# Latent attention's sums of squares: the rotated channels' squares are added before the matmul with ones

## The chip, the cores and the metric

The kernel runs on one core of one Trainium2 chip. Everything is float32; large weights are split into a high and a low part, and three matmuls (high by high, low by high, high by low) stand for one float32 product. The metric is the device time of one launch in microseconds (us). The kernel before took 1195.99 us as the median of three runs (1193.62 to 1198.3).

## The reference, cut to what matters

Two transformer layers over 256 tokens of 1024 channels. The part that is changed lies in the first layer's latent attention. Each of eight heads has queries and keys of 192 channels, 128 plain ones ("nope") and 64 that are rotated ("rope"), and each 192-vector is normalised before the rotation:

```
q_b = (rms_norm(cq, mla_cq_norm) @ w_uq).reshape(B, S, MLA_HEADS, MLA_QK_DIM)
k_b = concatenate([k_nope, broadcast_to(kr[:, :, None, :], (B, S, MLA_HEADS, MLA_ROPE_DIM))], axis=-1)
q_b = rms_norm(q_b, mla_q_norm)      # y = x * rsqrt(mean(x*x over 192) + 1e-6) * gain
k_b = rms_norm(k_b, mla_k_norm)
```

So each head and token needs one sum of 192 squares for the query and one for the key. The 64 rotated key channels are the same for all heads.

## The kernel before, in words

The program is written out by hand, engine by engine, in order. `latent_pe`, `latent_act`, `latent_dve` and `latent_pool` are the programs of TensorE, ScalarE, VectorE and GpSimd for the stage; what ties them together are semaphores (`wait_ge`, `then_inc`) and rings of buffers, where taking a buffer waits for the reader that had it last. Two rings of PSUM banks serve TensorE: `G` (three banks) for the projections, `M` (four banks) for the small products. Two SBUF rings of two buffers hold squares: `sq_ring` for the plain channels, `zt_ring` for the rotated query channels.

The stage has channels on partitions and tokens along the free dimension. A head pair `p` (0 to 3) has its plain channels in a tile of 128 partitions by 2 x 256 (two heads side by side), and its rotated channels in `mqr[:, p, :]`, 128 x 256: the even head's 64 channels on partitions 0 to 63, the odd head's on 64 to 127. The key's rotated squares `sqkr` are 128 x 256 with the same 64 channels in both halves.

TensorE goes through two loops of four turns:

- First loop, turn `half`: twelve matmuls of the key projection (`("ukv", 0)`, `mm_fm`, line 392), in turn 1 also the small product of `value_pe` (line 885), then the permutation for the rotation of query pair `half` (line 1109), then the sums of squares of query pair `half` (`mla_stat_pe`, lines 1131 and 1132).
- Second loop: twelve matmuls of the value projection (`("ukv", 1)`, `mm_tm`, line 410), then the sums of squares of key pair `half`. After the loop `ada_sums_pe(pe, 10)` (line 581), and then the next stage begins with 32 instructions of narrow scores (line 1489) and the gate projections (line 392).

ScalarE, for the query: squares the rotated channels (line 1178) and the plain ones (`mla_sq_act`, line 1140) of pair `half`, then turns the sums of pair `half - 1` into reciprocal roots (`mla_rstd_act`, Ln on line 1149, Exp on line 1151), then copies the key projection out of PSUM (line 1183). Between the loops it splits the next weights, of which the high part is written on line 344 (`next_hi(act, ("ukv", 1))`, which is the split of `("win", 7)`). In the second loop: square of key pair `half`, roots of the pair before, copy of the values (line 1191).

VectorE rotates the queries (lines 1237 to 1242), multiplies by the roots (lines 1248 to 1264), copies `value_pe`'s result (line 892), writes the low part of the split weights (line 351), and sums a modulation block (`ada_dve(dve, 10)`, lines 562 and 565). GpSimd has nothing to do in this stage before: its tables are made earlier, and its next instruction, a memset, waits for the stage's last `m_rope`.

A sum over partitions is a matmul with a matrix of ones. Before, each pair's sums take four float32 products of 256 columns, which accumulate in PSUM: for each of the two heads one of `ones` with the plain squares and one of `ones_lo` or `ones_hi` (ones on one half of the partitions) with the rotated squares.

Of the kernel before, what the change touches and what calls it, by code (L numbers as in the profile page):

```python
# [7 lines left out]
ALU = mybir.AluOpType  # L8
# [23 lines left out]
PT_, NPAR = _param_table()  # L32
CT_ = {}
NCON = 0
for _n, _k in [("ident", 128), ("ones_lo", 128), ("ones_hi", 128), ("perm64", 128), ("perm32", 128),
               ("cos", 256), ("sin", 256), ("cosr", 256), ("sinr", 256), ("mask2", 256), ("tri", 256),
               ("cadd", 30), ("cmul", 30), ("fold", 32)]:
    CT_[_n] = (NCON, _k)
    NCON += _k
# [108 lines left out]
def build(nc, ins, out):  # L148
# [130 lines left out]
    cmp_mm, cmp_set = sig("cmp_mm"), sig("cmp_set")  # L279
    ev_act, ev_dve = sig("ev_act"), sig("ev_dve")  # L280
    half_done = sig("half_done")
    m_sq, m_stat, m_nope, m_rope = sig("m_sq"), sig("m_stat"), sig("m_nope"), sig("m_rope")
    gt_exp, gt_set, gt_turn = sig("gt_exp"), sig("gt_set"), sig("gt_turn")
    cmp_sc, cmp_max, cmp_p, cmp_w = sig("cmp_sc"), sig("cmp_max"), sig("cmp_p"), sig("cmp_w")
# [775 lines left out]
    def latent_pe(pe):  # L1060
# [34 lines left out]
        for half in range(4):  # L1095
            b, old = G.take(ev_act("ukv", 0, half))
            if old:
                pe.wait_ge(*old)
            where["ukv", 0, half] = b
            mm_fm(pe, ("ukv", 0), ckvn, normed("vw") if half == 0 else held, b, half * 256,  # L1100
                  done=unit.hit("ukv", 0) if half == 3 else half_done.hit("ukv", 0, half))
            if half == 1:
                value_pe(pe)
            pm, old = M.take(rope_b("mq", half))
            if old:
                pe.wait_ge(*old)
            where["pm", "mq", half] = pm
            pe.wait_ge(*ev_act("uq", 2, half // 2))
            pe.matmul(pm[:, 0:256], cc("perm32"), mqr[:, half, :], start=True, stop=True).then_inc(
                perm_done.hit("mq", half), 1)  # L1110
            mla_stat_pe(pe, "mq", half, where["sqr", half][:, 0:256], ("ones_lo", "ones_hi"))
        for half in range(4):
            b, old = G.take(ev_act("ukv", 1, half))
            if old:
                pe.wait_ge(*old)
            where["ukv", 1, half] = b
            mm_tm(pe, ("ukv", 1), ckvn, held, b, half * 256, 256,
                  unit.hit("ukv", 1) if half == 3 else half_done.hit("ukv", 1, half))
            mla_stat_pe(pe, "mk", half, sqkr, ("ones_lo", "ones_lo"))
        ada_sums_pe(pe, 10)  # L1120

    def mla_stat_pe(pe, n, p, rsq, ones2):

        sm, old = M.take(rs_ln(n, p))
        if old:
            pe.wait_ge(*old)
        where["sm", n, p] = sm
        pe.wait_ge(*m_sq(n, p))
        sq = where["msq", n, p]
        for j in range(2):  # L1130
            pe.matmul(sm[:, j * 256:j * 256 + 256], ones[:], sq[:, j * 256:j * 256 + 256], start=True, stop=False)  # L1131
            ins_ = pe.matmul(sm[:, j * 256:j * 256 + 256], cc(ones2[j]), rsq, start=False, stop=True)
        ins_.then_inc(m_stat.hit(n, p), 1)

    def mla_sq_act(act, n, p, nope):
        buf, old = sq_ring.take(m_stat(n, p))
# [16 lines left out]
    def latent_act(act):  # L1153
# [16 lines left out]
        next_hi(act, ("ukv", 0))  # L1170
        hidden_act(act, 1)
        for half in range(4):
            buf, old = zt_ring.take(m_stat("mq", half))
            if old:
                act.wait_ge(*old)
            where["sqr", half] = buf
# [90 lines left out]
    def latent_pool(pool):  # L1267
        table_pool(pool, "mq", "mq_rope", "mq_rsw", "cosr", "sinr")
        table_pool(pool, "mk", "mk_rope", "mk_rsw", "cosr", "sinr")


    class Job:
# [1312 lines left out]
def _consts():  # L2585
    f = np.float32
# [5 lines left out]

    p = np.arange(128)
    put("ident", np.eye(128))
    put("ones_lo", (p < 64).astype(f)[:, None] * np.ones((1, 128), f))
    put("ones_hi", (p >= 64).astype(f)[:, None] * np.ones((1, 128), f))
    for n, h in (("perm64", 64), ("perm32", 32)):
        m = np.zeros((128, 128), f)
        m[p ^ h, p] = 1.0
# [158 lines left out]
```

## Time and profile before

| | us |
|---|---|
| median of three runs | 1195.99 |
| the profiled execution | 1199.0 |
| its span on the core | 1197.7 |
| TensorE busy | 1139.8 (95%) |
| VectorE busy | 748.5 (62%) |
| ScalarE busy | 590.9 (49%) |
| GpSimd busy | 25.9 (2%) |

The engine names in the rows are PE (TensorE matmul), PEld (its weight load), DVE (VectorE), ACT (ScalarE) and POOL (GpSimd). A matmul's duration in a timeline holds its way through the array, so that neighbours overlap; what one costs in a dense stretch is read from start to start, or from the chain of waits. A float32 product appears as two instructions. PEclk is the granted TensorE clock, 1.00 for 2.4 GHz and 0.50 for 1.2 GHz.

### The profile page before, as it was taken

How to read it: one execution, taken by the hardware profiler on the slowest of the kernel's cores; microseconds unless marked ns; L12 is line 12 of the kernel's file. 1: busy time of each engine (PE TensorE's matmuls, PEld its weight loads, DVE VectorE, ACT ScalarE, POOL GpSimd, SP SyncE). 2: the span in 40 equal slices, each digit the busy share in tenths (PEclk: the TensorE clock that was granted, in tenths of full speed). 3: DMA queues.
4: the chain of work that ended last, by engine and by line, in shares of the span. 5: the costliest groups of instructions: out<-in, count | busy, mean ns of one | idle time of the engine just before them, and what ended most of it. 6: DMA issues, size and time to landing. Idle time of an engine off the chain costs nothing.

```text
span 1197.7 us, 19285 instructions
## 1 busy us (share of the span) xinstructions
PE 1139.8 (95%) x7802; PEld 1033.5 (86%) x7802; DVE 748.5 (62%) x1411; ACT 590.9 (49%) x1043; POOL 25.9 (2%) x32
## 2 busy tenths in 40 slices
PE   7999699899899999999999899999999999999998
PEld 6987579788779999888988699998878978999986
DVE  2546546788658788765656666666455556666644
ACT  3455346444456666435325464444455357444533
POOL 0240000000000000001000000000000000000000
PEclk8999889899999999999989899999999989999999
DMA  7954563255144555564532275554545313655450
GB/s 310 384 187 179 219 247 141 92 199 212 62 141 159 179 187 193 183 248 173 195 108 102 70 267 195 191 177 159 193 146 178 116 62 130 214 181 189 141 193 36
DMA packets 30796, 207.81 MB, mean 174 GB/s; under 512 B 3539, under 2 KB 4051, under 8 KB 7156
## 3 DMA queue, kind: packets, MB, share of 16 engines
q1 hardware_dynamic: 30708, 206.58, 48.4%
q8 instruction: 62, 1.02, 0.3%
q14 instruction: 26, 0.21, 0.0%
HBM read 205.52 MB, written 1.05 MB: 172 GB/s over the span
## 4 chain that ended last, share of the span: by engine, by line
PE 84%; DVE 8%; ACT 4%; issue 2%; DMA 1%; SPq 0%; ACTq 0%; DVEq 0%
PE ps L392 47%; PE ps L1630 18%; PE ps L622 3%; PE ps L410 2%; DVE wlo L351 2%; DVE tm L565 1%; ACT whi L344 1%; PE ps L2231 1%; PE ps L2263 1%; DMA raw<-ada 1%; PE ps L1329 1%; PE ps L1755 1%; PE ps L581 1%; PE ps L1131 1%; PE ps L1407 1%
## 5 line engine op out<-in xcount | busy, mean ns | idle before, releaser
L351 DVE TENSOR_TENSOR wlo<-raw,whi 128x1024 fp32r<-128x1024 f32 (+2 forms) x328 | 370.3, 1171 | 253.3 <-ACT whi L344 253.1
L392 PE MATMUL ps<-H_h,whi 128*128 128x256 f32 x1552 | 447.9, 289 | 5.5 <-DVE wlo L351 5.5
L392 PE MATMUL ps<-H_l,whi 128*128 128x256 f32 x1552 | 442.5, 285 | 0.0
L392 PE MATMUL ps<-H_h,wlo 128*128 128x256 f32 x1552 | 442.3, 285 | 0.0
L344 ACT ACTIVATE whi<-raw 128x1024 fp32r<-128x1024 f32 (+2 forms) x328 | 315.5, 1010 | 184.8 <-PE ps L1630 111.9
L392 PEld LDWEIGHTS ps<-H_h,whi 128*128 128x128 f32 x1552 | 301.4, 194 | 10.4 <-issue 10.2
L392 PEld LDWEIGHTS ps<-H_l,whi 128*128 128x128 f32 x1552 | 301.4, 194 | 0.4 <-issue 0.2
L392 PEld LDWEIGHTS ps<-H_h,wlo 128*128 128x128 f32 x1552 | 301.2, 194 | 0.0
L1630 PE MATMUL ps<-whi,gl_h 128*128 128x512 f32 x264 | 105.6, 400 | 0.5 <-DVE wlo L351 0.5
L1630 PE MATMUL ps<-whi,gl_l 128*128 128x512 f32 x264 | 104.7, 396 | 0.0
L1630 PE MATMUL ps<-wlo,gl_h 128*128 128x512 f32 x264 | 104.6, 396 | 0.0
L1853 ACT ACTIVATE uw<-uw 128x256 f32<-128x256 f32 x66 | 27.4, 415 | 86.4 <-DVE uw L1944 86.4
L1630 PEld LDWEIGHTS ps<-whi,gl_h 128*128 128x128 f32 x264 | 49.7, 188 | 13.4 <-DVE wlo L351 1.4
L1630 PEld LDWEIGHTS ps<-wlo,gl_h 128*128 128x128 f32 x264 | 49.7, 188 | 12.1
L1630 PEld LDWEIGHTS ps<-whi,gl_l 128*128 128x128 f32 x264 | 49.7, 188 | 11.6
L1892 DVE SCALAR_TENSOR_TENSOR uw<-ps,par_sb,uw 128x255 f32<-128x255 f32 (+1 forms) x88 | 36.4, 475 | 25.2 <-ACT uw L1841 25.2
L1841 ACT ACTIVATE uw<-ps,par_sb 128x256 f32<-128x256 f32 x44 | 22.5, 562 | 46.5 <-PE ps L392 46.5
L565 DVE SCALAR_TENSOR_TENSOR tm<-raw,cs,tm 128x256 f32<-128x256 f32 x96 | 40.5, 477 | 0.0
L622 PE MATMUL ps<-H_h,whi 128*128 128x256 f32 x96 | 28.7, 299 | 4.9 <-DVE wlo L351 4.4
L1944 DVE TENSOR_TENSOR uw<-ps,rn 128x512 f32<-128x512 f32 x44 | 30.1, 684 | 2.2 <-PE ps L392 2.0
L1863 ACT ACTIVATE gl_h<-tm 128x256 fp32r<-128x256 f32 x66 | 27.5, 417 | 2.7 <-DVE tm L1859 2.7
L622 PE MATMUL ps<-H_l,whi 128*128 128x256 f32 x96 | 28.2, 294 | 0.0
(445 smaller groups left out, 1527.3 us busy)
## 6 DMA issues: line engine op xcount, KB each, us to landing
raw<-f SPq DMA_DIRECT2D x44, 1024.0 KB, 4.9
raw<-win SPq DMA_DIRECT2D x27, 1024.0 KB, 6.7
raw<-ada SPq DMA_DIRECT2D x24, 1024.0 KB, 5.8
raw<-up SPq DMA_DIRECT2D x22, 1024.0 KB, 4.8
raw<-g SPq DMA_DIRECT2D x20, 1024.0 KB, 4.9
raw<-pw SPq DMA_DIRECT2D x12, 1024.0 KB, 4.9
raw<-down SPq DMA_DIRECT2D x10, 1024.0 KB, 4.9
raw<-wa SPq DMA_DIRECT2D x4, 1024.0 KB, 9.6
```

What stands on the lines that cost most here:

```text
L344: act.activation(whi[j % NS][:, a:b], raw_of(key)[:, a:b], ACT.Copy).then_inc(w_hi.hit(key, half), 1)
L351: dve.tensor_tensor(wlo[j % NS][:, a:b], raw_of(key)[:, a:b], whi[j % NS][:, a:b].bitcast(F32), ALU.subtract).then_inc(w_lo.hit(key, half), 1)
L392: ins_ = pe.matmul(bank[:, m * 256:(m + 1) * 256], wt[a][:, kt * w + col + m * 128:kt * w + col + m * 128 + 128], act[b][:, k0 + kt, :], s ...
L410: ins_ = pe.matmul(bank[:, t * width:(t + 1) * width], act[b][:, kt, t * 128:(t + 1) * 128], wt[a][:, kt * w + col:kt * w + col + width], ...
L565: dve.scalar_tensor_tensor(out=o, in0=w, scalar=cs[:, kt:kt + 1], in1=o, op0=ALU.mult, op1=ALU.add).then_inc(ada_sum.hit(u, kt), 1)
L622: ins_ = pe.matmul(where["win", name][:, m * 256:(m + 1) * 256], wt[a][:, c:c + 128], H[b][:, k, :], start=k == 0 and m == 0 and i == 0, s ...
L1630: ins_ = pe.matmul(b[t][:], act[h][:, k0 + kt, t * 128:(t + 1) * 128], wt[a][:, kt * 512:(kt + 1) * 512], start=k0 + kt == 0 and i == 0 an ...
L1841: act.activation(w[:, m, :], z[:, m, :], ACT.Identity, bias=pc("b_conv", 2 * c + m), scale=pc("w_conv", (2 * c + m) * 3 + 2)).then_inc(u_i ...
L1853: act.activation(w[:, g, :], w[:, g, :], ACT.Silu).then_inc(u_silu.hit(n, c), 1)
L1863: act.activation(gl[0][:, c, :], where["tm", n, c][:, 0:256], ACT.Copy).then_inc(g_hi.hit(n, c), 1)
L1892: dve.scalar_tensor_tensor(out=w[:, m, s:], in0=z[:, m, 0:256 - s], scalar=pc("w_conv", (2 * c + m) * 3 + 2 - s), in1=w[:, m, s:], op0=ALU ...
L1944: dve.tensor_tensor(uw[c % 3][:], v2(where[n, c][:]), bc2(rn[:]), ALU.mult).then_inc(u_rn.hit(n, c), 1)
```

## The change

A new program part on GpSimd, `mla_add_pool`, adds the rotated squares onto the plain ones in place, for the even head on partitions 0 to 63 and for the odd head on 64 to 127: two additions of 64 x 256 for each pair, eight pairs. TensorE then needs one float32 product of 512 columns with `ones` for a pair in place of four of 256, and it asks for `m_add` (GpSimd's) in place of `m_sq` (ScalarE's). Each pair's product stands one turn later than before, key pair 3's behind `ada_sums_pe(pe, 10)`. The rotated query squares' buffers are free again when GpSimd has read them. Two constant matrices fall away, 256 columns of the constant table.

```diff
-for _n, _k in [("ident", 128), ("ones_lo", 128), ("ones_hi", 128), ("perm64", 128), ("perm32", 128),
+for _n, _k in [("ident", 128), ("perm64", 128), ("perm32", 128),
...
@@ latent_pe, first loop
-            mla_stat_pe(pe, "mq", half, where["sqr", half][:, 0:256], ("ones_lo", "ones_hi"))
+            if half:
+                mla_stat_pe(pe, "mq", half - 1)
@@ second loop
-            mla_stat_pe(pe, "mk", half, sqkr, ("ones_lo", "ones_lo"))
+            mla_stat_pe(pe, *(("mk", half - 1) if half else ("mq", 3)))
         ada_sums_pe(pe, 10)
+        mla_stat_pe(pe, "mk", 3)
...
-    def mla_stat_pe(pe, n, p, rsq, ones2):
+    def mla_stat_pe(pe, n, p):
...
-        pe.wait_ge(*m_sq(n, p))
-        sq = where["msq", n, p]
-        for j in range(2):
-            pe.matmul(sm[:, j * 256:j * 256 + 256], ones[:], sq[:, j * 256:j * 256 + 256], start=True, stop=False)
-            ins_ = pe.matmul(sm[:, j * 256:j * 256 + 256], cc(ones2[j]), rsq, start=False, stop=True)
-        ins_.then_inc(m_stat.hit(n, p), 1)
+        pe.wait_ge(*m_add(n, p))
+        pe.matmul(sm[:], ones[:], where["msq", n, p][:], start=True, stop=True).then_inc(m_stat.hit(n, p), 1)
+
+    def mla_add_pool(pool, n, p):
+
+        sq, r = where["msq", n, p], sqkr if n == "mk" else where["sqr", p][:, 0:256]
+        pool.wait_ge(*m_sq(n, p))
+        for a, b in ((0, 0), (64, 256)):
+            ins_ = pool.tensor_tensor(sq[a:a + 64, b:b + 256], sq[a:a + 64, b:b + 256], r[a:a + 64, :], ALU.add)
+        ins_.then_inc(m_add.hit(n, p), 1)
@@ latent_act
-            buf, old = zt_ring.take(m_stat("mq", half))
+            buf, old = zt_ring.take(m_add("mq", half))
@@ latent_pool
+        for n in ("mq", "mk"):
+            for p in range(4):
+                mla_add_pool(pool, n, p)
```

How TensorE's queue stands at the end of the first loop's turn 1. Before, with `sq1` the plain and `zt1` the rotated squares of query pair 1, `ps` a PSUM bank and `con_sb` the table with the half ones:

```order
L885 MATMUL ps1<-cw21_112,hid2_125 15x128 x3
L1109 MATMUL ps5<-mqr_93,con_sb_50 128x256 [waits ev_act,rs_ln]
L1131 MATMUL ps6<-sq1_68,ones_54 128x256 [waits m_sq,cmp_hid]
L1132 MATMUL ps6<-zt1_76,con_sb_50 128x256
L1131 MATMUL ps6<-sq1_68,ones_54 128x256
L1132 MATMUL ps6<-zt1_76,con_sb_50 128x256
L392 MATMUL ps2<-ckvn_h_121,whi1_62 128x256 [waits w_lo,ev_act]
```

The same place now:

```order
L886 MATMUL ps1<-cw21_112,hid2_125 15x128 x3
L1110 MATMUL ps4<-mqr_93,con_sb_50 128x256 [waits ev_act,gt_set]
L1132 MATMUL ps5<-sq0_67,ones_54 128x512 [waits m_add,rs_ln]
L393 MATMUL ps2<-ckvn_h_121,whi1_62 128x256 [waits w_lo,ev_act]
L393 MATMUL ps2<-ckvn_l_122,whi1_62 128x256
```

Four products of pair 1 have become one, twice as wide, and it is pair 0's (`sq0`). At the end of the stage, before:

```order
L1131 MATMUL ps6<-sq1_68,ones_54 128x256 [waits m_sq,rs_ln]
L1132 MATMUL ps6<-arow0_82,con_sb_50 128x256
L1131 MATMUL ps6<-sq1_68,ones_54 128x256
L1132 MATMUL ps6<-arow0_82,con_sb_50 128x256
L581 MATMUL ps2<-tm0_71,ones_54 128x256 [waits ada_sum,ev_act]
L581 MATMUL ps2<-tm1_72,ones_54 128x256
L1489 MATMUL ps3<-kcn_98,q_87 128x15 [waits rope_set,cmp_set,rs_ln]
```

and now:

```order
L1132 MATMUL ps5<-sq0_67,ones_54 128x512 [waits m_add,rs_ln]
L582 MATMUL ps2<-tm0_71,ones_54 128x256 [waits ada_sum,ev_act]
L582 MATMUL ps2<-tm1_72,ones_54 128x256
L1132 MATMUL ps6<-sq1_68,ones_54 128x512 [waits m_add,rs_ln]
L1499 MATMUL ps3<-kcn_98,q_87 128x15 [waits rope_set,cmp_set,rs_ln]
```

Key pair 3's product has moved behind the modulation sums (line 581 before, 582 now) and stands directly in front of the next stage. ScalarE's and VectorE's queues keep their order. GpSimd's has, between the tables and the memset, sixteen additions, of which the first four rows are:

```order
L1139 TENSOR_TENSOR sq0_67<-sq0_67,zt0_75 64x256 [waits m_sq]
L1139 TENSOR_TENSOR sq0_67<-sq0_67,zt0_75 64x256
L1139 TENSOR_TENSOR sq1_68<-sq1_68,zt1_76 64x256 [waits m_sq]
L1139 TENSOR_TENSOR sq1_68<-sq1_68,zt1_76 64x256
```

Each pair's first addition waits for ScalarE's square of the plain channels; nothing stood there before.

## Rows read from the trace of the kernel before

**Rows 1.** The page's parts on busy time and on granted clock, whole span

```profile
PE 1139.8 (95%) x7802; PEld 1033.5 (86%) x7802; DVE 748.5 (62%) x1411; ACT 590.9 (49%) x1043; POOL 25.9 (2%) x32
...
PEclk8999889899999999999989899999999989999999
```

**Rows 2.** Busy time by stretch: start:end, length, engines, clock, DMA share, GB/s

```profile
170.00:180.00 10.00, 10.00 (x64) 8.90 (x63) 6.79 (x17) 6.33 (x13) 0.00 (x0) 1.00 0.61 253
180.00:190.00 10.00, 10.00 (x65) 9.32 (x64) 9.48 (x20) 8.70 (x14) 0.00 (x0) 1.00 0.00 1
202.00:203.00 1.00, 1.00 (x6) 1.00 (x6) 0.93 (x4) 0.00 (x0) 0.00 (x0) 0.50 0.00 0
```

**Rows 3.** The chain that ended last: start us, us, engine, line

```profile
172.78 0.98 PE ps L885 x8
173.76 0.63 PE ps L1109 x2
174.38 0.43 PE ps L1131 x2
174.82 0.43 PE ps L1132 x2
...
176.11 1.41 PE ps L392 x12
...
196.76 3.48 PE ps L1489 x32
```

**Rows 4.** The same chain, earlier: a product of 512 columns with ones

```profile
109.77 0.86 PE ps L760 x2
```

**Rows 5.** Timeline of ScalarE: start, us, line, operation, idle before

```profile
173.31 0.41 ACT L1178 ACTIVATE zt<-mqr 128x256 f32<-128x256 f32 x1
173.62 0.62 ACT L1140 ACTIVATE sq<-mq 128x512 f32<-128x512 f32 x1
176.15 0.69 ACT L1149 ACTIVATE rst<-ps,epst 128x512 f32<-128x512 f32 x1 [1.91 <-PE ps L1132]
176.87 0.63 ACT L1151 ACTIVATE rst<-rst 128x512 f32<-128x512 f32 x1
177.56 0.60 ACT L1183 ACTIVATE mk<-ps 128x512 f32<-128x512 f32 x1
...
181.64 2.00 ACT L344 ACTIVATE whi<-raw 128x1024 fp32r<-128x1024 f32 x2
183.53 0.62 ACT L1140 ACTIVATE sq<-mk 128x512 f32<-128x512 f32 x1
```

**Rows 6.** Timeline of TensorE, the first of the sums

```profile
169.39 0.67 PE L1131 MATMUL ps<-sq,ones 128*128 128x256 f32 x2 [0.45 <-ACT sq L1140]
```

**Rows 7.** Timeline of VectorE in the stage

```profile
170.53 0.22 DVE L839 TENSOR_TENSOR hid<-ps,hid 128x60 f32<-128x60 f32 x1
...
180.33 0.41 DVE L892 COPY vcp<-ps 15x256 f32<-15x256 f32 x1
...
183.92 2.36 DVE L351 TENSOR_TENSOR wlo<-raw,whi 128x1024 fp32r<-128x1024 f32 x2
```

**Rows 8.** Timeline of GpSimd, its operations on SBUF data

```profile
55.61 2.04 POOL L1031 TENSOR_SCALAR tab_qc<-con_sb,par_sb 128x256 f32<-128x256 f32 x1
57.63 1.43 POOL L1032 TENSOR_SCALAR tab_qs<-con_sb,par_sb 128x256 f32<-128x256 f32 x1
59.04 0.92 POOL L1031 TENSOR_SCALAR tab_ksc<-con_sb,par_sb 128x256 f32<-128x256 f32 x1
...
73.06 5.42 POOL L1040 TENSOR_TENSOR xb<-xc,par_sb 128x240 f32<-128x240 f32 x8 [10.38 <-DVE xc L775]
...
81.13 2.53 POOL L1032 TENSOR_SCALAR tab_mks<-con_sb,par_sb 128x256 f32<-128x256 f32 x1
```

**Rows 9.** Timeline of VectorE beside GpSimd's operations

```profile
54.58 3.77 DVE L351 TENSOR_TENSOR wlo<-raw,whi 128x1024 fp32r<-128x1024 f32 x4 [2.73 <-ACT whi L344]
...
80.59 2.36 DVE L351 TENSOR_TENSOR wlo<-raw,whi 128x1024 fp32r<-128x1024 f32 x2 [7.62 <-ACT whi L344]
```

More of the change, by code:

```diff
@@ L281, in build @@
     half_done = sig("half_done")
+    m_add = sig("m_add")
     m_sq, m_stat, m_nope, m_rope = sig("m_sq"), sig("m_stat"), sig("m_nope"), sig("m_rope")
@@ L2594, in _consts @@
     put("ident", np.eye(128))
-    put("ones_lo", (p < 64).astype(f)[:, None] * np.ones((1, 128), f))
-    put("ones_hi", (p >= 64).astype(f)[:, None] * np.ones((1, 128), f))
     for n, h in (("perm64", 64), ("perm32", 32)):
```

## The prediction

> **What bounds the kernel now.** I read the page first: TensorE is busy for 1139.8 of 1197.7 us [rows 1], so the whole program is bound by TensorE, and GpSimd is nearly empty (25.9 us). Then the stretches of the stage: from 170 to 190 us TensorE has no idle time and runs at the full 2.4 GHz, VectorE is busy for 6.79 and then 9.48 of 10 us, ScalarE for 6.33 and then 8.70 [rows 2]. The DMA share falls to nothing, with no wait for a load: the weights are there. The chain of waits shows that the path goes straight through TensorE's queue here, sums of squares included: four products of 0.43 us to a pair, the twelve projection matmuls 1.41 us (up to 1.44 in other turns), the permutation 0.43 us (0.63 behind the small product), the small product 0.98 us [rows 3]. So time taken from TensorE here is time of the kernel, as long as nobody else is late for it. ScalarE is the one to look at: it waits for TensorE's sums (1.91 us at 176.15) [rows 5], so it has some slack, but its slack is small where its share is 8.7 of 10.
>
> **What is removed.** A pair's sums cost 4 x 0.43 = 1.72 us of TensorE before. A product of 512 columns with ones costs 0.86 us [rows 4], and that is the shape that the change uses. Eight pairs: 8 x (1.72 - 0.86) = 6.9 us. The first sum waited 0.45 us for ScalarE's square [rows 6]; it now stands one turn later, so this wait goes too. Together 7.35 us leave TensorE's queue. If nothing else changed, that would be the gain.
>
> **What is added.** Two GpSimd additions of 64 x 256 for each pair, between ScalarE's square and TensorE's product. No row has this shape. From below: eight additions of 240 columns took 5.42 us, 0.68 each, which makes 0.72 for 256 columns and 1.45 for a pair, with a handover some 1.5 us [rows 8]. From above: one operation of 256 columns took 2.53 us, so a pair could take 5.1 us. In between, a quiet operation of 256 columns took 0.92 us, while two in a row beside VectorE's weight split took 2.04 and 1.43, 3.5 us for a pair [rows 8, 9]. In those two stretches VectorE was in back-to-back subtractions with both inputs in SBUF; in the stage that is changed it is busy for 7 to 9.5 of 10 us, but mostly with operations of 0.4 to 0.75 us. I take 2.1 us for a pair: the additions' own 1.45, 0.1 for the handover and 0.25 to 0.3 of holding off for each, nearest to the quiet rows.
>
> The Trainium skill, SBUF — State Buffer, section "SBUF: two separate sides", states that a VectorE instruction with two SBUF inputs and a GpSimd instruction that reads SBUF share one port pair which is an exclusive lock, so that one fully blocks while the other runs. The trace agrees in direction: 2.53 us against 0.92 [rows 8], beside a VectorE split of 2 x 1.18 us [rows 9]. By that rule in its full form the forecast would be the slower rival below.
>
> **Where the new cover is too thin.** I follow TensorE from the end of the first permutation (168.9 us: the first sum started at 169.39 after 0.45 of waiting) with the old durations and 2.1 us for a pair of additions.
>
> 1. Turn 1: twelve matmuls end at 170.3. `value_pe` needs `hid`, which VectorE finishes at 170.75 [rows 7], a time that the change does not move. A wait of 0.6 us that the longer sums used to cover. Pair 0's product ends at 173.2.
> 2. The loop that now closes through four engines: TensorE's product, ScalarE's roots (1.42 us from 176.15 to 177.56), its copy (0.5), its squares (0.31 and 0.62) [rows 5], GpSimd's pair (2.1 with handovers), the next product but one (0.86): 5.9 us for two turns. TensorE's own work in two turns is 2 x (1.43 + 0.43 + 0.86) = 5.4. The first time that this bites is pair 2: 0.5 us.
> 3. The second loop's first turn takes the PSUM bank that `value_dve` must have read (VectorE line 892, at 180.33 before [rows 7]); this stands behind the multiplication of query pair 1, which needs pair 1's roots (ready about 177.3), and so ends about 179.35: 0.3 us of waiting. Pair 3's product then 0.1.
> 4. Key pair 0 is the large one. Its square stands on ScalarE behind the split of the next weights, 1.9 us (181.64 to 183.53) [rows 5]. Pair 2's product ends at 179.1, roots to 180.55, copy to 181.05, split to 183.0, square to 183.6, additions to 185.8. TensorE arrives at 183.3. A wait of 2.5 us. With additions of 1.5 us it is 1.5 us.
> 5. Key pair 1 fits (0.1). Key pair 2: pair 0's product ends at 186.7, plus 1.42, 0.5, 0.62 and 2.1 makes 191.4, TensorE is there at 190.5: 0.95. Key pair 3: 189.05 plus the same makes 193.8, TensorE has finished line 581 at 193.15: 0.65.
>
> Waits: 0.6 + 0.5 + 0.3 + 0.1 + 2.5 + 0.1 + 0.95 + 0.65 = 5.7 us. The narrow scores of line 1489, at 196.76 before [rows 3], begin 7.35 - 5.7 = 1.65 us earlier. The same walk with 1.5 us for a pair of additions gives waits of 4.0 and a gain of 3.4; with 2.5 us the waits are about 7.0 and the gain is 0.3; with 3.4 us the loops run at GpSimd's pace, waits 11.2, a loss of 3.8.
>
> **Behind the stage.** ScalarE's split for the second gate projection follows key pair 3's roots and a table load, and VectorE's half of it that; TensorE first has 3.48 us of narrow scores and a whole gate projection in front, so this does not become late. GpSimd's memset has the same place behind the last `m_rope`. The next stages are the same instructions 1.65 us earlier. Dropping 256 columns of the constant table makes one early load smaller, long before this stage: nothing. The zt buffers are freed by GpSimd rather than TensorE, earlier than ScalarE asks: nothing.
>
> **The sum.** The profiled execution took 1199.0 us (span 1197.7), 3 us above the median of 1196.0; its stage becomes 1.65 shorter, and I take the same difference from the median: 1194.3 us.
>
> **The rivals.**
> - *All of it arrives.* If the additions were done whenever TensorE asks, the gain would be 6.9 to 7.35 less the 0.6 at `hid`: about 6.5 us, 1189.5. For it: TensorE 100% busy, GpSimd empty. Against it: key pair 0's square behind the split, which even free additions would meet only just. Chance 0.1.
> - *GpSimd is held off by VectorE.* The mechanism is that of the 55 to 59 us stretch: each addition waits while a two-input VectorE operation runs, a pair costs 3.4 us or more, and in both loops TensorE waits for `m_add` in nearly every turn. From 2.6 us a pair on the change loses. At 3.4 us it is 3.8 us slower, 1199.8; at 4.1 us, halfway to the upper bound, 8.1 us slower, 1204. For it: from 180 to 190 us VectorE is busy for 9.48 of 10 us, and its weight split of 2.36 us stands there [rows 2, 7]. Against it: from 170 to 180 it is idle for 3.2 of 10, between short operations, and it loses time itself to GpSimd, which would move it apart. Chance 0.27, of which 0.12 lie over 1202.
> - *The clock falls.* TensorE's granted clock fell to 0.50 at 202 us behind 3.48 us of narrow scores [rows 2, 3]. The new 2.5 us of idle time at 183 might do the same. Three us at half rate cost 1.5 us, of which part disappears in the waits that are there anyway: 1195.5. Chance 0.13.
>
> **How the numbers follow.** The forecast itself (a gain of 0.5 to 4 us) has 0.5. Its own range is 1192 to 1195.7. The range that should hold 8 times in 10 reaches down to the case in which all arrives (1189.5) and up into the contention case, 1201.5. Half a per cent, 6 us, is what a measurement of this kernel can tell from no change. Faster than 1190.0: the first rival, 0.1. Slower than 1202: the part of the second, 0.12. The same: 0.78.
>
> **What would show it.** In the changed kernel's profile: eight sums of 0.86 us on the chain; the GpSimd additions with 0.7 to 1.1 us each (right) or over 1.6 (the contention rival); TensorE's idle time in front of line 1132 released by GpSimd, 4 to 6 us in total with the largest, 1.5 to 2.5 us, at key pair 0, and one of 0.6 in front of the small product; line 1499 starting 1 to 3.5 us before 196.76. If no wait for GpSimd stands at key pair 0, step 4 is wrong; if the scores start earlier but the span does not follow, the part behind the stage is.

## The result, and the profile after

The change made the kernel slower: 1199.9 us as the median of 19 runs (1194.3 to 1205.7) against 1196.7 us for the kernel before (19 runs, 1193.6 to 1200.1), a ratio of 1.0029 with a 95% interval of 1.0019 to 1.0040. By that ratio, which is used from here on, it is 3.5 us slower. The forecast was 1.65 us faster.

TensorE did lose the work. The page of the profiled execution of the changed kernel, busy time:

```profile
PE 1131.5 (95%) x7754; PEld 1021.6 (86%) x7754; DVE 754.3 (63%) x1411; ACT 590.5 (49%) x1043; POOL 40.7 (3%) x48
```

Against [rows 1], TensorE is busy for 8.3 us less, GpSimd for 14.8 us more, and VectorE, whose queue did not change by one instruction, for 5.8 us more.

The profiled execution happens to be the fastest of the 19 (1194.3 us, span 1193.0). It is 4.8 us ahead of the old trace when the stage begins and 3.3 us ahead when it ends. So the stage has to be read by itself. I measure it from the start of the first permutation to the start of the narrow scores: 28.26 us before (168.34 to 196.60), 29.75 us now (163.52 to 193.27). What TensorE waited for in it, in the changed kernel (us in total, times, longest):

```profile
PE ps L1132 <- POOL sq L1139: 3.9, 2, 2.3
PE ps L411 <- DVE vcp L893: 1.4, 1, 1.4
PE ps L886 <- DVE hid L840: 1.1, 1, 1.1
```

That is 6.4 us of waits, where before there was one of 0.45 [rows 6]. The forecast had 5.7: 0.6 for `hid`, 0.3 for the value copy and 4.8 for GpSimd over six products. The last came to 3.9 at two of them, 2.28 us at key pair 0 and 1.60 at key pair 3.

The waits alone don't make the stage longer: with 6.9 us of work gone and 6.4 us of waits for 0.45 it should be 0.95 us shorter, and it is 1.5 us longer. Of the 2.4 us in between, some 1.7 are TensorE at 1.2 GHz for 3.4 us from 182.8 on, right behind the wait at key pair 0; the last column but two is the granted clock, in the changed kernel:

```profile
180.00:185.00 5.00, 2.72 (x9) 1.68 (x8) 5.00 (x8) 2.12 (x5) 3.70 (x4) 0.78 0.00 0
185.00:190.00 5.00, 5.00 (x27) 3.90 (x26) 4.91 (x10) 3.38 (x7) 1.96 (x2) 0.88 0.55 193
```

This is the place at which the prediction's third rival has the clock fall. The other 0.7 us are small pieces: pair 2's product starts 0.2 us late, and a product behind a wait takes longer, key pair 3's 1.10 us for 0.86.

That says how TensorE's time is filled, not what sets it. The chain that ended last shows what the forecast had not seen. In the changed kernel, where line 352 is the weight split, 563 and 566 the modulation block, 1255 to 1259 the multiplication of query pair 3, and 1156 and 1158 the roots:

```profile
178.84 2.89 DVE wlo L352 x2
181.74 1.53 DVE tm L563 x2
183.26 2.34 DVE tm L566 x5
...
186.16 0.67 DVE mq L1255
...
187.17 0.88 DVE mqr L1259
...
188.13 0.70 ACT rst L1156
...
189.97 0.53 ACT sq L1147
...
190.56 0.76 POOL sq L1139
...
192.34 1.10 PE ps L1132 x2
193.44 3.75 PE ps L1499 x32
```

The path no longer runs through TensorE, as in [rows 3]; from 170.6 to 188.1 us it runs through VectorE (the lines show it from 178.8 on), then through ScalarE and GpSimd to key pair 3's product. The link is one ScalarE row of the changed kernel:

```profile
188.13 0.69 ACT L1156 ACTIVATE rst<-ps,epst 128x512 f32<-128x512 f32 x1 [1.59 <-DVE mqr L1259]
```

`mla_rstd_act` takes its result buffer from a ring of two. Key pair 1's roots need the buffer that query pair 3 had, and VectorE frees that one only behind the weight split and the modulation block. The same wait stood in the trace before, where it cost nothing because TensorE was still busy. In the kernel before:

```profile
190.70 0.69 ACT L1149 ACTIVATE rst<-ps,epst 128x512 f32<-128x512 f32 x1 [1.69 <-DVE mqr L1252]
```

And VectorE itself has become slower. In the changed kernel, at the same three operations:

```profile
178.84 2.89 DVE L352 TENSOR_TENSOR wlo<-raw,whi 128x1024 fp32r<-128x1024 f32 x2
181.66 1.60 DVE L563 TENSOR_SCALAR tm<-raw,cs 128x256 f32<-128x256 f32 x2
183.18 2.97 DVE L566 SCALAR_TENSOR_TENSOR tm<-raw,cs,tm 128x256 f32<-128x256 f32 x6
```

Before, the split took 2.36 us [rows 7], the scalings 0.61 and the sums 2.46: 2.0 us more, all beside GpSimd's additions for key pairs 0 and 1, which took 4.73 us for four. Two of the query pairs took 1.64 and 1.67 us:

```profile
171.91 1.64 POOL L1139 TENSOR_TENSOR sq<-sq,zt 64x256 f32<-64x256 f32 x2 [3.66 <-ACT sq L1147]
174.62 1.67 POOL L1139 TENSOR_TENSOR sq<-sq,zt 64x256 f32<-64x256 f32 x2 [1.07 <-ACT sq L1147]
179.16 4.73 POOL L1139 TENSOR_TENSOR sq<-sq,arow 64x256 f32<-64x256 f32 x4 [2.87 <-ACT sq L1147]
```

So there are four candidates: the hop through GpSimd (an engine more between square and sum), the sum's place one turn later, the time for which GpSimd and VectorE hold each other off, and TensorE's low clock.

### The profile page after: what moved, and what is told of

Its sections match the earlier page's. It is cut to its first block, busy times and chain, and to the rows that moved or that the text cites. A ratio compares the mean times of both kernels' runs of the same rounds, so it can differ in the third digit from the quotient of the medians.

```text
span 1193.0 us, 19205 instructions
## 1 busy us (share of the span) xinstructions
PE 1131.5 (95%) x7754; PEld 1021.6 (86%) x7754; DVE 754.3 (63%) x1411; ACT 590.5 (49%) x1043; POOL 40.7 (3%) x48
## 3 DMA queue, kind: packets, MB, share of 16 engines
HBM read 205.39 MB, written 1.05 MB: 173 GB/s over the span
## 4 chain that ended last, share of the span: by engine, by line
PE 83%; DVE 9%; ACT 4%; issue 2%; DMA 1%; POOL 0%; SPq 0%; ACTq 0%; DVEq 0%
PE ps L393 47%; PE ps L1640 19%; PE ps L623 3%; DVE wlo L352 2%; PE ps L411 2%; DVE tm L566 1%; ACT whi L345 1%; PE ps L2241 1%; PE ps L2273 1%; PE ps L1339 1%; PE ps L1765 1%; PE ps L1417 1%; PE ps L582 1%; DMA raw<-ada 1%; PE ps L434 1%
## 5 line engine op out<-in xcount | busy, mean ns | idle before, releaser
L393 PE MATMUL ps<-H_l,whi 128*128 128x256 f32 x1552 | 440.9, 284 | 0.0
L1640 PE MATMUL ps<-whi,H_h 128*128 128x512 f32 x64 | 26.2, 410 | 2.2 <-DVE wlo L352 1.9
```

The source lines that it names most:

```text
L393: ins_ = pe.matmul(bank[:, m * 256:(m + 1) * 256], wt[a][:, kt * w + col + m * 128:kt * w + col + m * 128 + 128], act[b][:, k0 + kt, :], s ...
L1640: ins_ = pe.matmul(b[t][:], act[h][:, k0 + kt, t * 128:(t + 1) * 128], wt[a][:, kt * 512:(kt + 1) * 512], start=k0 + kt == 0 and i == 0 an ...
```

## The experiments

Each was timed with the kernel before on the same chip. "Stage" is the stretch defined above, from the experiment's profile, which is a single execution. Ratios are to the kernel before; most rest on 12 runs, three moves without additions and the spin on five, scores first on six. Where the intervals of two experiments overlap widely, the difference between them is not settled.

| kernel | stage, us | ratio | 95% interval |
|---|---|---|---|
| before | 28.26, 28.25 | 1 | |
| changed | 29.75, 30.80, 29.75, 29.72 | 1.0029 | 1.0019 to 1.0040 |
| no additions | 24.09 | 0.9972 | 0.9951 to 0.9992 |
| later place only | 28.72 | 1.0011 | 0.9994 to 1.0029 |
| additions beside | 32.46 | 1.0035 | 1.0018 to 1.0051 |
| additions of 8 columns | 24.79 | 0.9978 | 0.9964 to 0.9992 |
| square first | 31.17 | 1.0054 | 1.0037 to 1.0072 |
| multiplication first | 29.31 | 1.0013 | 0.9998 to 1.0029 |
| both first | 27.73 | 0.9977 | 0.9959 to 0.9996 |
| value product too | 26.93 | 0.9979 | 0.9965 to 0.9992 |
| three moves, no additions | 22.02 | 0.9942 | 0.9930 to 0.9954 |
| three moves on before | 28.22 | 0.9997 | 0.9983 to 1.0012 |
| three moves, queries only | 25.53 | 0.9986 | 0.9971 to 1.0002 |
| spin | 31.19 | 1.0061 | 1.0044 to 1.0078 |
| scores first | (22.80) | 0.9954 | 0.9940 to 0.9969 |

### No additions

```diff
@@ the changed kernel, mla_stat_pe; GpSimd's calls are gone
-        pe.wait_ge(*m_add(n, p))
+        pe.wait_ge(*m_sq(n, p))
```

> The changed kernel without the GpSimd additions: TensorE sums the plain channels' squares alone with its one product of 512 columns, one turn late, and waits for ScalarE's square again. The rotated squares are left out of the sums. Chain theory (what eats the gain is the new hop through GpSimd: 3.9 us of waits for it at key pairs 0 and 3, a turn of low clock behind the first of them, and VectorE's delays at value_dve): without the hop the stage is 4 to 6 us shorter than before, so the kernel is 3.5 to 6 us faster than before, near 1191 us. Deferral theory (the product one turn late is what makes ScalarE and VectorE late, GpSimd or not): still no faster than 1 us against before. In its trace the chain theory expects no wait over 1 us in front of key pair 0's product.

The stage took 24.09 us, 5.7 less than changed and 4.2 less than before; the kernel 0.9972 (3.4 us faster). The additions cost about 5.7 us of the stage; without them 4.2 of the 6.9 us that TensorE saves arrive there. At key pair 0 TensorE doesn't wait, as expected. Three waits are left: 0.5 us for `hid`, 0.7 for the value copy, and 1.65 right in front of key pair 3's product, for ScalarE's square. The last is there without any GpSimd: with each product a turn later, sum, roots, copy and square follow one another, and step 5 of the prediction had 0.65 us for it, additions included. Since the later place is in this kernel and it is faster than before, the later place alone can't be what makes the change slower.

### The later place only

```diff
@@ the kernel before: all four products, one turn later
-            mla_stat_pe(pe, "mq", half, ...)
+            if half:
+                mla_stat_pe(pe, "mq", half - 1, ...)
```

> The kernel before with nothing changed but the place of the sums: all four products of a pair, one turn later, key pair 3's behind the modulation sums; no GpSimd. Chain theory: TensorE's turns stay long enough to cover ScalarE, waits under 1 us in total, so within 1 us of before. Deferral theory: 2 to 4 us slower than before.

28.72 us for the stage, 0.5 more than before, one wait of 1.0 us at `value_pe`; 1.0011, not told apart from 1. Taken alone this doesn't exclude the deferral theory, since the interval reaches 3.5 us; in the stage the later place costs 0.5 us, and the run without additions rules it out as the whole cause.

### Additions beside

```diff
@@ the kernel before; the sums use sq and r as they were
+            ins_ = pool.tensor_tensor(scr[a:a + 64, :], sq[a:a + 64, b:b + 256], r[a:a + 64, :], ALU.add)
```

> The kernel before, with GpSimd doing the sixteen additions into a scratch buffer that nobody reads; TensorE's products and their waits stay as they were, only the squares' buffers wait for GpSimd too. Contention theory (GpSimd and VectorE hold each other off, and VectorE's delay is what costs): 2 to 3 us slower than before, with VectorE's split at key pair 0 near 2.9 us for 2.4 and its two scalings near 1.6 us for 0.6. Chain theory: the same delays show on VectorE, but TensorE has no new wait over 1 us, and the kernel is within 1 us of before.

The result nobody reads, and still the stage is 4.2 us longer and the kernel slower by 0.35% (4.2 us), as much as the real change. The chain theory as I had written it (no new wait, within 1 us) falls: the interval begins at 2.2 us, and TensorE waits 2.5 us for a square of ScalarE's behind the delay. The contention theory had 2 to 3 us. On VectorE the split took 3.32 us, the scalings 1.60 and the sums 3.42 (before 2.36, 0.61, 2.46), and ScalarE's wait for VectorE grew to this, in the kernel with the additions beside:

```profile
189.69 0.69 ACT L1153 ACTIVATE rst<-ps,epst 128x512 f32<-128x512 f32 x1 [5.15 <-DVE mqr L1258]
```

It is not quite free of a hop, for the squares' buffers wait for GpSimd too. But in its trace no engine's idle time in the stage ends with GpSimd. So holding off is enough to cost as much as the change does; that it is all, this run doesn't show.

### Additions of 8 columns

```diff
@@ the changed kernel, mla_add_pool
-            ... sq[a:a + 64, b:b + 256], sq[a:a + 64, b:b + 256], r[a:a + 64, :], ALU.add)
+            ... sq[a:a + 64, b:b + 8], sq[a:a + 64, b:b + 8], r[a:a + 64, 0:8], ALU.add)
```

> The changed kernel with additions of 8 columns instead of 256, same instructions, same waits (most of the rotated squares are left out of the sums). Port theory (what costs is the time for which a GpSimd addition and a VectorE operation with SBUF inputs hold each other off): VectorE's split, scalings and sums return to 2.3, 0.5 and 2.4 us, and the stage is within 1.5 us of the 24.1 us without additions, kernel 2 to 3.5 us faster than before. Hop theory (dispatch and semaphores through a fourth engine): each pair still costs over 1 us, the stage stays over 27 us, kernel no faster than before.

This separates the hop from the holding off: same instructions, same semaphores, same order, 1/32 of the data. The stage took 24.79 us, 0.7 more than without additions, and the kernel was 0.9978. VectorE was back at its old durations, in the kernel with 8 columns:

```profile
180.06 2.37 DVE L352 TENSOR_TENSOR wlo<-raw,whi 128x1024 fp32r<-128x1024 f32 x2
182.34 0.60 DVE L563 TENSOR_SCALAR tm<-raw,cs 128x256 f32<-128x256 f32 x2
182.87 2.46 DVE L566 SCALAR_TENSOR_TENSOR tm<-raw,cs,tm 128x256 f32<-128x256 f32 x6
```

Of the 5.7 us that the additions cost in the stage, about 0.7 is the hop as such and 5.0 goes with the additions' length: their own running time in the loop and what they and VectorE take from each other. How the 5.0 divides between these two no run shows. The Trainium skill, SBUF — State Buffer, section "SBUF: two separate sides", gives the form of it: one port pair for both, locked for a whole instruction. The rows of the changed kernel and of this one agree with it for the split, which has two SBUF inputs. For operations with a single tensor input, such as the scalings, the section names a 2-port performance mode; whether they ran in it, and which lock hit which instruction, no view shows.

### Square first

```diff
@@ the changed kernel, latent_act
+        act.wait_ge(*ev_act("ukv", 0, 0))
+        mla_sq_act(act, "mk", 0, mk[:, 0:2, :])
         next_hi(act, ("ukv", 1))
```

> The changed kernel with key pair 0's square put ahead of the 1.9 us weight split on ScalarE. Chain theory: the 2.3 us wait for GpSimd in front of key pair 0's product goes and so does the low clock behind it, 2 to 4 us faster than the changed kernel, which makes it equal to the kernel before or up to 1 us faster. Contention theory: the addition meets VectorE's work anyway and the wait moves to the next pair: within 1 us of the changed kernel, that is 2 to 3 us slower than before.

A miss for both: the obvious cure for the largest wait made the stage 1.4 us longer, and the kernel has 1.0054. The wait at key pair 0 did go (TensorE ran on to 181.95 us without one), and TensorE, early, then stood 1.30 us in front of key pair 1's product and 4.45 us in front of key pair 3's. ScalarE's row in this kernel says why:

```profile
188.45 0.69 ACT L1156 ACTIVATE rst<-ps,epst 128x512 f32<-128x512 f32 x1 [5.14 <-DVE mqr L1262]
```

With the square first, the pace is VectorE's: what was gained at key pair 0 came back as one long idle stretch before the narrow scores. Of the 1.4 us that the stage lost, 0.5 are VectorE's, whose sums now stand beside the additions for key pairs 1 and 2 (3.46 us for 2.97). The rest is key pair 3's product, which ran at 1.2 GHz behind the idle stretch, 2.05 us for 1.10.

### Multiplication first, and both

```diff
@@ the changed kernel, latent_dve
-        ada_dve(dve, 10)
-        ... mq_norm_dve(dve, 3) behind it, in the loop
+        mq_norm_dve(dve, 3)
+        ada_dve(dve, 10)
```

> The changed kernel with one move on VectorE: the multiplication of query pair 3 by its roots stands ahead of the modulation block (ada_dve 10), not behind it. VectorE theory (the roots of key pair 1 need the buffer that VectorE frees with query pair 3, and VectorE gets there only behind the weight split and the modulation block, both of which GpSimd stretches): ScalarE's 1.6 us wait for VectorE at 188 us goes, the last product comes 0.5 to 1.5 us earlier, the kernel is 0.5 to 2 us faster than the changed one. Hop theory (only GpSimd's own 1.6 us and the low clock count): no difference from the changed kernel.

> Both moves: key pair 0's square ahead of ScalarE's weight split, and query pair 3's multiplication ahead of VectorE's modulation block. VectorE theory: the square's move alone made the kernel slower only since ScalarE's 5.1 us wait for VectorE came into view; with both the waits of TensorE in the second loop fall under 3 us, the granted clock stays at full, and the kernel is 6 to 9 us faster than with the square's move alone, 1 to 3 us faster than before. Hop theory: key pairs 0 and 1 are held up by the port as before, at least 4 us of waits for GpSimd stay, and the kernel is at best as fast as before.

Alone, the multiplication of query pair 3 ahead of the modulation block gave 1.0013. That is 1.9 us better than changed, but the intervals overlap, and the stage is only 0.4 us shorter than 29.75. ScalarE's 1.59 us wait is gone, and the chain that ended last now runs through the other wait, at key pair 0, with the low clock behind it. In the kernel with the multiplication first:

```profile
178.87 1.50 POOL sq L1139
...
180.43 1.62 POOL sq L1139
...
182.18 1.91 PE ps L1132 x2
184.09 2.22 PE ps L411 x12
```

At full clock the last two took 1.10 (behind a wait) and 1.43. So two chains are about equally late in the changed kernel, the one through VectorE and the ring and the one through key pair 0, and a cure for either alone gives little or nothing. With both cures the kernel has 0.9977: faster than before by 2.8 us and than the square alone by 9.2. The square's move costs about 3 us in one order and gives 4.3 in the other. The clock stayed full in the stage, as expected; but TensorE still waits 1.4 us for the value copy, 1.6 for VectorE at the modulation sums and 1.6 for GpSimd from the second loop on, 4.6 us where the expectation had under 3.

### The value product too, and without additions

```diff
@@ latent_pe, latent_dve, beside both moves
-            if half == 1:
+            if half == 2:
                 value_pe(pe)
...
+            if half == 3:
+                value_dve(dve)
             if half:
                 mq_norm_dve(dve, half - 1)
-            if half == 2:
-                value_dve(dve)
```

> As the kernel with both moves, and in addition the small value product stands in turn 2 and VectorE copies its result in turn 3 ahead of the multiplication, so that TensorE's two waits for VectorE (1.1 us for hid, 1.4 us for the copy in the changed kernel) should go. Expected by the VectorE theory: 1.5 to 3 us faster than with both moves, 3 to 5 us faster than before, near 1192 us. If GpSimd's additions are what paces the first loop, the time only moves to the next wait for them: within 1 us of the kernel with both moves.

> All three moves and no GpSimd additions (the rotated squares are left out of the sums, as in the first experiment). This is what the halved product is worth when nobody is late: both theories expect 6 to 8 us faster than before, near 1189 us. The distance to the same kernel with the additions is the price of the additions that order cannot hide: under 2 us by the VectorE theory, 3 us or more by the hop theory.

The value product's two waits went, the stage was 0.8 us shorter, the kernel was the same within the intervals (0.9979). The VectorE theory had 1.5 to 3 us more; what happened is the other case, for TensorE's waits for GpSimd rose from 1.6 to 2.9 us. Without additions the three moves give 22.02 us, 6.2 less than before, and 0.9942, 6.9 us faster than before (5.5 to 8.4): about all of the saved TensorE work. The additions' price with the three moves is 4.9 us in the stage and 0.37% (4.4 us) in the kernel, more than the 2 us that the VectorE theory had. It is the size that the hop theory named, but the additions of 8 columns speak against its mechanism: order hides only a part of what the additions' length costs.

### The moves on the kernel before, and the queries only

> The kernel before with the three moves alone (square of key pair 0 ahead of the split, query pair 3's multiplication ahead of the modulation block, value product a turn later), no GpSimd, four products for a pair. Both theories: TensorE was bound by its own work in this stage, so the moves alone give nothing, within 1 us of before. If this is faster by 2 us or more, the gain of the kernels with the moves is the moves' and not the halved sums'.

28.22 us and 0.9997. Without the halved sums no gain of the moves can be told (the interval allows 2 us at most).

```diff
@@ with the three moves, mla_stat_pe and latent_pool: key pairs as before
+        if n == "mq":
+            pe.wait_ge(*m_add(n, p)); one product of 512 columns; return
+        pe.wait_ge(*m_sq(n, p))
+        the four products of 256 columns
```

> The three moves, GpSimd additions and one product of 512 columns for the query pairs only; the key pairs keep their four products and wait for ScalarE. Port theory: half of the 6.9 us stays saved, and VectorE's split, modulation block and key multiplications run undisturbed; the stage takes 25 to 26.5 us, 0.5 to 2 us less than with all additions and the moves (26.9), kernel 2 to 4 us faster than before. Rival (the additions cost the same in both loops): stage 27 us or more, no faster than the kernel with all additions and the moves.

The stage was 25.53 us as expected, 1.4 less than with all additions; the kernel was 0.9986 (0.9971 to 1.0002), 1.7 us faster where 2 to 4 were expected, and its interval overlaps that of all additions with the moves. Not settled.

### Further executions of the changed kernel and of the kernel before

> The changed kernel unchanged, for a second profiled execution. The stage from the first permutation to the narrow scores took 29.75 us in the first one, 1.5 more than before, while the paired runs say 3.5 us for the whole. Clock theory: the stage repeats within 0.5 us but for the 3.4 us stretches at half clock, which fall in different numbers; the rest of the loss is such stretches, 1.7 us each. Stage theory: the stage itself varies, 30.5 to 32 us in other executions.

> As the run before it: a third profiled execution of the changed kernel, same expectations (stage 29.75 within 0.5 us by the clock theory, 30.5 to 32 us by the stage theory).

> A fourth profiled execution of the changed kernel, same expectations as the two before it.

> The kernel before, a second profiled execution. Both theories: 28.26 us for the stage within 0.2 us, no stretch at half clock inside it, and VectorE's split, scalings and sums at 2.28, 0.53 and 2.38 us.

The stage took 30.80, 29.75 and 29.72 us, and 28.25 in the kernel before. Two of three repeated; 30.80 is what the stage theory had. In that execution the clock stayed full inside the stage, and TensorE's waits came to 8.9 us instead. VectorE was 0.5 us later from `hid` on, so the multiplication of query pair 3 fell beside GpSimd's additions for key pair 2 and took 2.5 us for 2.0, and ScalarE waited 2.8 us for it rather than 1.6. That is the whole difference: from these roots to the scores both executions take 5.1 us, at low clock or at full. So VectorE's chain makes the stage long here and not the low clock inside it. What varies more is the clock behind the stage. The 15 us from the narrow scores on, TensorE's columns and PEclk, first in the kernel before (two executions, one fence each), then in four of the changed kernel:

```profile
196.00:211.00 15.00, 15.00 (x115) 14.92 (x113) 7.29 (x15) 7.32 (x9) 0.56 (x2) 0.89 0.34 135
```

```profile
193.50:208.50 15.00, 15.00 (x116) 14.95 (x115) 7.55 (x15) 7.05 (x9) 0.56 (x2) 0.89 0.31 127
```

```profile
193.00:208.00 15.00, 15.00 (x115) 14.76 (x114) 8.58 (x18) 7.38 (x9) 0.56 (x2) 0.89 0.35 132
```

```profile
195.50:210.50 15.00, 15.00 (x88) 14.76 (x87) 5.52 (x10) 5.09 (x6) 0.56 (x2) 0.66 0.32 120
```

```profile
195.00:210.00 15.00, 15.00 (x102) 14.85 (x101) 7.11 (x15) 6.89 (x9) 0.56 (x2) 0.77 0.34 131
```

```profile
193.00:208.00 15.00, 15.00 (x103) 14.91 (x102) 7.12 (x16) 6.97 (x9) 0.56 (x2) 0.77 0.35 131
```

TensorE is busy throughout in all six, but gets through 115 and 116 instructions before and 115, 88, 102 and 103 now. In three of the four, the clock stands at 1.2 GHz for longer than before. All four have 1.6 us or more of idle time shortly before the narrow scores, and the kernel before has none. But the idle time isn't shown to be the reason. The kernel with the later place only has none in the last 25 us before its scores, and its mean clock in the same 15 us is 0.77; the kernel with both moves has 1.6 us of it, and 0.89. Without additions the clock is 0.77, with additions of 8 columns 0.66. What sets it stays open. Measured from the first permutation to VectorE's first gating of the attention output (line 1560 before), both effects are in: 64.2 and 64.1 us before; 65.0, 69.8, 67.2 and 67.2 now, on average 3.2 us more, of which 1.75 are the stage and 1.4 what stands behind it. With four executions and two that fits the 3.5 us of the runs, but it is no more than an account: how often the clock falls for how long isn't known from so few.

### Spin

```diff
@@ the changed kernel, in front of key pair 0's wait for m_add
+            for _ in range(5):
+                pe.matmul(sm[:, 0:256], cc("ident"), con[:, 0:256], start=True, stop=True)
```

> The changed kernel with five products of the identity into the sum's bank in front of key pair 0's wait for GpSimd (2.1 us of TensorE work at full clock, overwritten by the sum): the wait stays, but TensorE is not idle in it. Clock theory: the granted clock no longer falls at 183 us, scores 1.5 to 2 us earlier, kernel 1 to 2 us faster than the changed one. Rival: the engines behind are late anyway (VectorE's end sets the pace), and the low clock costs nothing: within 0.5 us of the changed kernel.

> The spin kernel a second time for an undisturbed profile (the first one ran at half clock throughout). Clock theory: no stretch at half clock between key pair 0's product and the scores. If the kernel is slow all the same, the stage shows why: the spin's 2.1 us is longer than the wait that it fills and delays the product, 30 us or more to the scores.

1.0061, with square first the slowest. The profile of the second execution shows the clock at full through the products of the second loop, and at 0.58 in the 15 us behind, in this kernel:

```profile
178.00:190.00 12.00, 10.87 (x58) 7.95 (x56) 11.86 (x19) 6.89 (x13) 6.42 (x6) 1.00 0.24 87
190.00:205.00 15.00, 12.40 (x52) 11.40 (x53) 8.63 (x14) 7.08 (x10) 2.10 (x4) 0.58 0.54 209
```

The low clock inside the stage costs little in this order, for TensorE is not its pace: without it the stage was no shorter (31.19 us), and a wait of 2.9 us stood at key pair 3's product, as in the execution of 30.80. As there, the multiplication of query pair 3 met an addition of GpSimd's (2.5 us for 2.0). The clock theory, which had the scores 1.5 to 2 us earlier, falls. Behind the stage the low clock costs, since TensorE is busy there throughout; no run changes it alone.

### Scores first

```diff
@@ with all additions and the three moves; latent_pe and attn_pe
-        ada_sums_pe(pe, 10)
-        mla_stat_pe(pe, "mk", 3)
...
         ins_.then_inc(cmp_sc.hit(), 1)
+        ada_sums_pe(pe, 10)
+        mla_stat_pe(pe, "mk", 3)
+        free = list(M.free)
         gate_pe(pe, 0)
```

> All additions and the three moves, and in addition the modulation sums and key pair 3's product stand behind the narrow scores, not in front of them. Port and clock theory: the 1.6 us wait for VectorE at the modulation sums goes, the scores come 2 to 3 us earlier than with the three moves, the half-clock stretch behind them stays at 3.4 us; 1 to 3 us faster than with the three moves, 3.5 to 5 us faster than before, near 1192 us. Rival: VectorE, still stretched by the additions, becomes the wait of the next stage (its split for the second gate projection), and the time stays where the three moves have it.

0.9954 (0.9940 to 0.9969): 5.5 us faster than before, 3.0 faster than with the three moves, and the best kernel of the study with the whole computation. The narrow scores need neither the modulation sums nor key pair 3, so they fill the time in which VectorE and GpSimd finish. (Its stage of 22.80 us leaves those two out and isn't comparable; to the first gating it is 60.7 us, against 62.8 with the three moves and 64.1 before.) TensorE's waits, in this kernel:

```profile
PE ps L1131 <- POOL sq L1138: 2.4, 3, 1.4
PE ps L1131 <- ACT rst L1155: 0.6, 1, 0.6
```

## Why the prediction was wrong

**The removed work: right.** Four products of 0.43 us became one of 0.86; with hardly a wait left the saving arrives in full (three moves, no additions: 6.9 us). The first sum's 0.45 us wait went too.

**The additions: their size nearly right, their effect on the others missing.** I took 2.1 us for a pair; the eight took 1.93 on average, from 1.63 to 2.4. But the sum charged the holding off to GpSimd alone. VectorE's 2.0 us over split, scalings and sums was in no term, though the rule that the prediction takes from the Trainium skill, SBUF — State Buffer, section "SBUF: two separate sides", has whichever side comes second blocked, and the sum should have had a line for the other side. With additions of 8 columns those 2.0 us and all but 0.7 of the 5.7 us went.

**Steps 1 and 3, the waits at `hid` and at the value copy: right in place, too small** (1.1 us for 0.6, 1.4 for 0.3). VectorE, from which both come, was held off as well; without additions they are 0.5 and 0.7. Step 2's 0.5 us at pair 2 was 0.2 (its terms add up to 5.8 us rather than 5.9, which makes it 0.4).

**Step 4, key pair 0: right** (2.3 us for 2.5), and yet not the binding wait. Square first removed it, and the stage became longer.

**Step 5 is the step that failed, and the missing term is why its size was off.** It walked key pairs 1 to 3 through TensorE, ScalarE and GpSimd and never asked which buffer the roots go to. The ring's two buffers tie key pair 1's roots to VectorE's multiplication of query pair 3. ScalarE's wait for it, 1.69 us, stood in the trace before, but the prediction's rows of ScalarE end at 183.5 us [rows 5]. With the split and the modulation block 2.0 us longer in front of that multiplication, the path went through VectorE. Key pair 2's 0.95 us of waiting did not come, key pair 3's came to 1.6 for 0.65, and the stage ended 1.5 us later than before where the forecast had it 1.65 earlier. Of these 3.15 us the waits are only 0.7; the rest is the low clock behind key pair 0 (1.7 us) and small pieces (0.7). But that low clock only fills time that VectorE's chain sets: in the execution without it the stage is 1.05 us longer, and from ScalarE's late roots to the scores it is 5.1 us in both.

**Behind the stage: wrong.** "The next stages are the same instructions earlier" is true of the instructions, not of the clock: in three of four executions TensorE ran longer at 1.2 GHz behind the scores than before, 1.4 us on average. Why is open. The clock rival (1.5 us, chance 0.13) named key pair 0. There the clock did fall, in three of four executions and for 1.7 us of TensorE's time, but most of it was hidden behind VectorE's chain; for the place where it costs there was no term.

**The rivals.** The contention rival named the mechanism, and its time for 3.4 us a pair (1199.8) is close to the 1199.9 measured. That is luck: it let TensorE wait for `m_add` in nearly every turn, where the additions took 1.93 us a pair, TensorE waited at two products, and the loss works through VectorE. Of the listed signs, GpSimd's additions of 0.7 to 1.1 us and waits of 4 to 6 us pointed to the forecast. Most additions took that long (one took 1.61 us), the waits came to 3.9 us, and the kernel was slower all the same. Even the scores started 3.3 us before their old time, as the list has it, only because this execution entered the stage 4.8 us ahead: a start has to be read from the beginning of its stage. The signs were of the parts that I had priced, so they could not show what I had left out.

## What to carry to other kernels

When work leaves the bound engine, walk the new chain through every buffer ring too, and look for waits in the old trace that cost nothing then: the next bound may be one of them, as here. Where two chains are about equally late, a cure for one shows nothing; try both together. Work given to GpSimd beside a busy VectorE is paid by VectorE as well; price it with a copy of the work whose result nobody reads, and with one on a few columns, before trusting its own duration. Where some idle time must stay, fill it with independent products, as the narrow scores did here. What idle time ahead of thin work does to the clock behind it these runs don't settle, so profile more than one execution before reading a clock.

## What the runs showed of the hardware

- An addition of 64 x 256 float32 on GpSimd took 0.72 us at its shortest, about as long as 240 columns on all 128 partitions (0.72 to 0.73): half the partitions did not make it shorter here. Beside VectorE's split it took up to 1.61 us. Of 8 columns it took 0.20 to 0.54 us in the first loop and up to 1.09 us beside the split.
- VectorE's two scalings of 128 x 256, which have a single tensor input, went from 0.61 to 1.60 us beside the additions, relatively more than the operations with two tensor inputs (split 2.36 to 2.89, sums 2.46 to 2.97).
- With 8-column additions those three groups of VectorE's had their old durations to within 0.01 us.
- Four additions (4 x 0.72 = 2.9 us by their shortest) made VectorE's three groups 2.0 us longer and took 1.8 us longer themselves.
- In the spin kernel TensorE's granted clock was 1.00 through 12 us with 1.1 us of idle time and 0.58 on average in the following 15, with 2.6 us of idle time and the 32 narrow products. In all profiled executions read here but one the clock fell to 1.2 GHz between 2 us before and 5 us behind the start of the narrow scores; with the three moves and no additions it stayed full for 19 us behind it. How long it stays low differed between executions of one kernel, and why was not found.
